# GpSimd subtracts the lower parts of four weight units in VectorE's place

## The chip, the cores and the metric

One core of a Trainium2 chip runs one launch of the kernel. The metric is the device time of that launch in microseconds (us): the median over runs. The engines are called TensorE (PE in the profile), VectorE (DVE), ScalarE (ACT), GpSimd (POOL) and SyncE (SP, which only issues transfers here).

## The reference

Two transformer blocks in sequence over 512 tokens of width 1024, all in float32. The first has a causal pooling branch and a forgetting attention; it is not touched. The second, in which the change lies, is cut here to what matters:

```python
def stick_breaking_attention(q, k, v):           # 8 heads of 64, blocks of 128 queries
    ...
        z = einsum('bqhd,bkhd->bhqk', qb, kb) * scale
        log_beta = log_sigmoid(z)
        log_1m_beta = where(strict, log_sigmoid(-z), 0.0)
        suffix = cumsum(log_1m_beta, axis=3, reverse=True) - log_1m_beta
        w = where(strict, exp(log_beta + suffix), 0.0)
        outs.append(einsum('bhqk,bkhd->bqhd', w, vb))

def second_block(x, c, ...):
    ...
        proj = h @ w_in[l]                       # q, k, v of 8 stick-breaking and 8 chunked heads
        o_sb = stick_breaking_attention(...)
        o_ca = chunked_relpos_attention(...)
        mixed = concatenate([o_sb, o_ca], axis=-1)
        x = x + gt1 * (mixed @ w_o[l])
        h = rmsnorm_2(x, g_norm2[l]) * (1.0 + sc2) + sh2
        x = x + gt2 * (square(relu(h @ w1[l])) @ w2[l])
```

## The kernel before

Every large product is done in three matmuls on split operands: a float32 operand is written as an upper part (rounded to the format that TensorE multiplies) and a lower part (what the rounding left), and `three` (L2276 to L2278) adds upper times upper, upper times lower and lower times upper in one bank of PSUM.

The weights come in 88 units of 128 x 2048, numbered w. SyncE loads a unit into one of three raw buffers (`load`, L575). ScalarE makes the upper part in four chunks of 512 columns (`upper`, L733, semaphore `a["wh"]`), and VectorE subtracts it from the raw chunk to get the lower part (`lower`, L1318, semaphore `v["wl"]`, four counts a unit). There are two homes for the parts, so the upper part of unit w+2 waits until TensorE has read unit w. TensorE waits for the count of `v["wl"]` before the first product of a chunk, and SyncE waits for the fourth count of unit w before it loads another unit into that raw buffer.

Every engine's instructions stand in an order written out by hand. In the stage that matters, steps n run from 0 to 187, sixteen of them to a weight unit (W_CA = 30 at n = 0); in step n of odd index, `slot` puts the chunks of unit w+1 into ScalarE's and VectorE's orders (`UPPER` and `LOWER`, `uppers` and `lowers`). Between the products of the weights lie the "beats" of the attention heads: a score (L2423), its sigmoid on ScalarE (L879), the running product of sticks as a scan on VectorE (`sticks`, L1518, both operands in SBUF), the transposes on TensorE (L2450), the split of the transposed weights on ScalarE (L898) and VectorE (`turned`, L1537, one operand in PSUM), the products with the values (L2474, L2479), and the collection of the head's output (L907, L1548, L916, L1558). A transpose also waits until VectorE's `turned` has emptied its bank, two transposes back. Heads 16 to 23 are the stick-breaking ones.

Units 36 to 39 are the projections of the stick-breaking heads' queries and keys (n = 96 to 159) and units 40 to 43 the output projection (W_O = 40; units 40 and 41 from n = 160 on). Unit 44 is the first of the wide layer that follows.

GpSimd masks scores and loads tiles earlier; in this stage it clears some table corners, builds the strip of the scan (four small instructions up to L2221), and then waits until the last stick-breaking head's values are done (`t["value"]`, `n_turn(23, 0)`) and for ScalarE's sums of squares, to make the factors of the second normalisation (L2227, L2230). Its semaphore `rs1` counts twelve steps of the first normalisation (three for each of four blocks).

Of the kernel before, what the change touches and what calls it, by code (L numbers as in the profile page):

```python
# [17 lines left out]
EPS = 1e-6  # L18
# [121 lines left out]
def program(nc, x, xcols, wall, wf, poolw, params, fng, wada, crow_in, rel, out):  # L140
# [31 lines left out]
    with ExitStack() as ctx:  # L172
# [162 lines left out]

        g = sems("pool_", "const", "meta", "rs0", "rs1", "rs3", "mask", "bt", "strip")

# [160 lines left out]
        def upper_at(w, s_):  # L498
            return uppers.get(w, UPPER).get(s_, ()) if w + 1 < NW else ()

        def lower_at(w, s_):
            return lowers.get(w, LOWER).get(s_, ()) if w + 1 < NW else ()
# [68 lines left out]
        def _(e):  # L571
# [5 lines left out]
            def loads_to(last):  # L577
                while todo[0] <= min(last, W_MLP + 3):
                    n = todo[0]
                    todo[0] += 1  # L580
                    if n >= NR:
                        e.wait_ge(v["wl"], 4 * (n - NR) + 4)
                    load(n, place[n])
# [106 lines left out]
            for q in range(4):  # L690
                o, u, (a0, a1, a2, a3) = W_MLP + 11 * q, W_MLP + 8 * q, places[q]

                if q:
                    e.wait_ge(v["wl"], 4 * o + 4)
                load(u + 4 + 1, a0)
                e.wait_ge(v["wl"], 4 * (o + 1) + 4)
                load(u + 4 + 1, a1)
                e.wait_ge(v["wl"], 4 * (o + 2) + 4)
                load(u + 4, a2)
                e.wait_ge(v["wl"], 4 * (o + 3) + 4)  # L700
                load(u + 4 + 3, a3)
                e.wait_ge(v["wl"], 4 * (o + 5) + 4)
                load(u + 4 + 1, a3)
                if q < 3:
                    e.wait_ge(v["wl"], 4 * (o + 6) + 4)
                    load(u + 8, a0)
                    e.wait_ge(v["wl"], 4 * (o + 8) + 4)
                    load(u + 9, a2)
                    e.wait_ge(v["wl"], 4 * (o + 9) + 4)
                    load(u + 10, a3)  # L710
                    e.wait_ge(v["wl"], 4 * (o + 10) + 4)
                    load(u + 11, a1)
# [8 lines left out]
        def _(e):  # L721
# [312 lines left out]
            def keep(i):  # L1034
                e.wait_ge(g["rs1"], 3 * i + 3)
                e.activation(x1[:, i, :], scaled[:, i % 2, :], ACT.Copy, scale=sm[:, 128 + 2 * i:129 + 2 * i]).then_inc(a["xk"], 1)
# [277 lines left out]
        def _(e):  # L1314
            def lower(w, c):
                e.wait_ge(a["wh"], 4 * w + c + 1)
                upper_, lower_ = parts_at(w, c)
                e.tensor_tensor(lower_, raw_of(w, c), upper_.bitcast(F32), ALU.subtract).then_inc(v["wl"], 1)  # L1318
# [396 lines left out]
            def norms(i):  # L1715

                e.wait_ge(g["rs1"], 3 * i + 3)
                e.wait_ge(t["tp"], i) if i else e.wait_ge(v["ol"], 4)
                e.tensor_scalar(normed, scaled[:, i % 2, :], sm[:, 129 + 2 * i:130 + 2 * i], None,
                                ALU.mult).then_inc(v["xn1"], 1)  # L1720
# [371 lines left out]
        def _(e):  # L2092
# [98 lines left out]
            for i in range(4):  # L2191


                m1, m2 = sm[:, 120 + 2 * i:121 + 2 * i], sm[:, 121 + 2 * i:122 + 2 * i]
                r = sm[:, 128 + 2 * i:130 + 2 * i]
                e.wait_ge(a["nsq"], 2 * i + 1)
                e.tensor_scalar(r[:, 0:1], m1, EPS, None, ALU.add).then_inc(g["rs1"], 1)
                e.wait_ge(a["nsq"], 2 * i + 2)
                e.wait_ge(g["rs1"], 3 * i + 1)
                e.tensor_scalar(r[:, 1:2], r[:, 0:1], EPS, m2, ALU.mult, ALU.add).then_inc(g["rs1"], 1)  # L2200
                e.wait_ge(g["rs1"], 3 * i + 2)
                e.tensor_tensor(r, r, half[:, 0:2], ALU.pow).then_inc(g["rs1"], 1)
            gate(0)
# [3 lines left out]
            for h in CA:  # L2207
                e.wait_ge(d[f"bt{h % 2}"], 16 * (h // 2 - 3))
                e.memset(bt[h % 2][0:64, 448:512], NEG).then_inc(g["bt"], 1)
                if h == 9:  # L2210
                    for j in range(4):
# [9 lines left out]
            e.affine_select(out=strip[:, 384:512], in_=strip[:, 384:512], compare_op=ALU.is_ge, fill=0.0, base=0,  # L2221
                            pattern=[[1, 128]], channel_multiplier=-1).then_inc(g["strip"], 1)
            e.wait_ge(t["value"], n_turn(23, 0))
            for i in range(4):
# [25 lines left out]
            for q in range(4):  # L2250
                o, (a0, a1, a2, a3) = W_MLP + 11 * q + 4, places[q]
                o3, o2 = o + order(q).index(7), o + order(q).index(6)
                if q < 3:
                    e.wait_ge(d[f"w{place[o3]}"], 16 * n_load[o3])
                    add(q, 2, place[o3])
                e.wait_ge(d[f"w{place[o2]}"], 16 * n_load[o2])
                add(q, 2, place[o2])
                e.wait_ge(d[f"wa{place[o2]}"], 192 + 16 * n_add[o2] - 16)
                add(q, 0, place[o2])
                if q == 3:  # L2260
                    e.wait_ge(d[f"w{place[o3]}"], 16 * n_load[o3])
                    add(q, 2, place[o3])
                    to_residual("*c12")
                    to_residual("*c21")
                e.wait_ge(v["wl"], 4 * o + 4)
                add(q, 2, a2)
                e.wait_ge(v["wl"], 4 * o2 + 4)
                add(q, 3, place[o2])
                if q == 0:
                    gate(1)  # L2270
# [3 lines left out]
        def _(e):  # L2274
# [5 lines left out]
            def by_cols(w, sub, k, out_, c0, n, start, stop, fresh):  # L2280

                o = 256 * k + 128 * sub
                upper, lower = home(w)
                if fresh and k % 2 == 0:
                    e.wait_ge(v["wl"], 4 * w + k // 2 + 1)
                return three(out_, upper[:, o:o + 128], lower[:, o:o + 128], hh[:, k, c0:c0 + n],
                             hl[:, k, c0:c0 + n], start, stop)
# [287 lines left out]
            for ee in range(4):  # L2575
# [7 lines left out]
                for i in range(4):  # L2583
                    bank_free(8 * ee + 4 + i)
                    e.wait_ge(v["wl"], 4 * w + i + 1)
                    if ee == 0:
                        e.wait_ge(v["ol"] if i % 2 else v["yl"], 4)
                    for k in range(4):
                        o, kt = 512 * i + 128 * k, 4 * (i % 2) + k
                        ins = three(bank[up_bank(ee, i)], wh[:, w % NH, o:o + 128], wl[:, w % NH, o:o + 128],  # L2590
                                    ah[:, kt, :], al[:, kt, :], k == 0, k == 3)
                    ins.then_inc(t["up"], 1)


            for kh in range(2):
                w = W_OUT + kh
                for i in range(4):
# [4 lines left out]
                    for k in range(4):  # L2602
                        if i == 0:
                            e.wait_ge(v["wl"], 4 * w + k + 1)
                            e.wait_ge(v["ml"], 4 * kh + k + 1)
                        ins = by_rows(w, k, 4 * kh + k, bank[OUT_BANK[0][i]], (mh, ml), 128 * i, 128,
                                      kh == 0 and k == 0, kh == 1 and k == 3)
# [6 lines left out]
            def out_block(i):  # L2614
                if i == 0:
                    e.wait_ge(v["m"], 24)
                for kt in range(8):
                    w = W_OUT + 2 + kt // 4
                    if i == 0:
                        e.wait_ge(v["wl"], 4 * w + kt % 4 + 1)  # L2620
                    ins = by_rows(w, kt % 4, kt, bank[OUT_BANK[1][i]], (mh, ml), 128 * i, 128, kt == 0, kt == 7)
# [14 lines left out]
            def vca_block(i):  # L2636
                for kt in range(8):
                    w = W_VCA + kt // 4
                    if i == 0:
                        e.wait_ge(v["wl"], 4 * w + kt % 4 + 1)  # L2640
                    if kt % 4 == 0:
# [18 lines left out]
            for n in range(steps_s):  # L2660
# [11 lines left out]
                elif n < 96:  # L2672
# [4 lines left out]
                    if i == 0:  # L2677
                        e.wait_ge(v["wl"], 4 * w + kt % 4 + 1)
                    ins = by_rows(w, kt % 4, kt, bank[VSB_BANK[i]], (hh, hl), META + 128 * i, 128, kt == 0, kt == 7)
# [14 lines left out]
                else:  # L2694
# [4 lines left out]
                    if i == 0:  # L2699
                        e.wait_ge(v["wl"], 4 * w + kt % 4 + 1)  # L2700
                        e.wait_ge(v["ol"], 8 if kt > 3 else 9 + kt)
# [17 lines left out]
            e.wait_ge(v["ol"], 12)  # L2719
            e.wait_ge(v["wl"], 4 * (W_O + 1) + 4)  # L2720
            for i in range(4):
# [11 lines left out]
            def o_block(i):  # L2733
                if i == 1:
                    e.wait_ge(v["turn"], n_turn(23, 0))
                for n, kt in enumerate((4, 5, 6, 7, 0, 1, 2, 3)):
                    w = W_O + 2 + (kt < 4)
                    if i == 0:
                        e.wait_ge(v["wl"], 4 * w + kt % 4 + 1)
                    if i == 3 and n == 1:  # L2740
# [32 lines left out]
            def product(q, r):  # L2773
                p, w = ORDER[r], W_MLP + 11 * q + 4 + r
                upper, lower = home(w)
                for b in range(2):
# [5 lines left out]
                    for k in range(4):  # L2782
                        if b == 0:
                            e.wait_ge(v["wl"], 4 * w + k + 1)
                            e.wait_ge(v["sl"], n_sl(q, k if p in (1, 7) else 4 + k, p in (5, 6, 3)))
# [5 lines left out]
            def last_product(r):  # L2791
                p, w = LAST_ORDER[r], W_MLP + 37 + r
                for b in range(2):
# [12 lines left out]
                    for c0, c1 in HALVES[b] if p in (5, 3) else HALVES[0]:  # L2806
                        for k in range(4):
                            if b == 0:
                                e.wait_ge(v["wl"], 4 * w + k + 1)
                                e.wait_ge(v["sl"], n_sl(3, k if p in (1, 7) else 4 + k, p in (5, 6, 3)))  # L2810
# [79 lines left out]
```

## Time and profile before

| what | value |
|---|---|
| median of 3 runs | 955.28 us (955.16 to 955.39) |
| the profiled execution's own time | 955.42 us |
| its span, first to last instruction | 953.7 us |
| TensorE matmul busy | 941.1 us, 4712 instructions |
| VectorE busy | 691.2 us, 1278 instructions |
| ScalarE busy | 565.2 us, 1115 instructions |
| GpSimd busy | 103.8 us, 215 instructions |
| granted TensorE clock | 1.0 |

The page says which engine is busy in which part of the span; the chain of waits says what released what; a timeline gives one instruction a row, with its start and its duration. The durations of matmuls overlap (their ends are modelled), so TensorE is read from the starts of its instructions and from the idle time that the trace lists ahead of one. On VectorE and ScalarE an instruction is listed from its issue, and the next one's start can lie some 0.1 us before the end of the one ahead; back to back, 512-column subtractions start 0.60 us apart.

### The profile page before, as it was taken

To read this page: it belongs to the slowest core of one execution; us is meant where nothing else is said; L and a number is where in the kernel's file an instruction comes from. 1 tells how busy PE (TensorE), PEld (TensorE's weight loads), DVE (VectorE), ACT (ScalarE), POOL (GpSimd) and SP (SyncE) were. 2 spreads that over 40 slices of the span, in tenths; PEclk is the share of its full clock that TensorE was granted. 3 is DMA by queue.
4 is the path that set the end of the run, shared out by engine and by line. 5 is a ranking of instruction groups with operands and counts; after the bars stand their busy time and mean duration, and the time that the engine had idled before them with its cause. 6 is when DMAs were issued, how large, how long until landed. Compare 5 with 4: busy or idle time off the path is not lost.

```text
span 953.7 us, 13305 instructions
## 1 busy us (share of the span) xinstructions
PE 941.1 (99%) x4712; PEld 786.3 (82%) x4712; DVE 691.2 (72%) x1278; ACT 565.2 (59%) x1115; POOL 103.8 (11%) x215
## 2 busy tenths in 40 slices
PE   8999999999999999999999999999999999999998
PEld 7878998888888887877788877898888888888887
DVE  6487888878788766667768886856544853673988
ACT  6448787753223257479987664556745634644562
POOL 5001212211121103000000000110000000000110
PEclk9999999999999999999999999999999999999999
DMA  8233222149798743733442423365867567586773
GB/s 302 89 112 108 69 79 89 55 157 354 284 322 278 190 142 127 300 111 100 133 166 73 127 67 131 146 167 133 212 207 180 168 192 189 122 234 193 169 186 111
DMA packets 34963, 156.71 MB, mean 164 GB/s; under 512 B 5273, under 2 KB 5529, under 8 KB 22226
## 3 DMA queue, kind: packets, MB, share of 16 engines
q1 hardware_dynamic: 21106, 103.64, 31.6%
q0 software_dynamic: 11152, 49.29, 20.9%
q10 hardware_dynamic: 2640, 2.93, 0.9%
q8 instruction: 38, 0.62, 0.3%
q14 instruction: 27, 0.22, 0.1%
HBM read 144.61 MB, written 5.27 MB: 157 GB/s over the span
## 4 chain that ended last, share of the span: by engine, by line
PE 86%; DVE 9%; ACT 3%; issue 1%; DMA 1%; ACTq 0%; POOL 0%; DVEq 0%; POOLq 0%
PE psum L2276 26%; PE psum L2278 25%; PE psum L2277 25%; PE psum L2423 2%; PE psum L2450 2%; PE psum L2479 1%; PE psum L2474 1%; DVE wl L1318 1%; DVE p_sb L1518 1%; DMA raw<-in_wall 1%; DVE ptl L1537 1%; PE psum L2712 1%; DVE hl L1357 1%; DVE xt L1353 1%; DVE ah L1464 1%
## 5 line engine op out<-in xcount | busy, mean ns | idle before, releaser
L2276 PE MATMUL psum<-hh,wh 128*128 128x512 f32 (+2 forms) x736 | 277.7, 377 | 0.7 <-DVE hl L1357 0.6
L2278 PE MATMUL psum<-hh,wl 128*128 128x512 f32 (+2 forms) x736 | 270.2, 367 | 0.0
L2277 PE MATMUL psum<-hl,wh 128*128 128x512 f32 (+2 forms) x736 | 270.0, 367 | 0.0
L1318 DVE TENSOR_TENSOR wl<-raw,wh 128x512 fp32r<-128x512 f32 x336 | 218.7, 685 | 37.6 <-ACT wh L733 37.0
L733 ACT ACTIVATE wh<-raw 128x512 fp32r<-128x512 f32 x336 | 193.3, 621 | 68.3 <-PE psum L2278 65.2
L2276 PEld LDWEIGHTS psum<-hh,wh 128*128 128x128 f32 x736 | 138.5, 188 | 24.5 <-DVE hl L1357 1.8
L2278 PEld LDWEIGHTS psum<-hh,wl 128*128 128x128 f32 x736 | 138.4, 188 | 23.0
L2277 PEld LDWEIGHTS psum<-hl,wh 128*128 128x128 f32 x736 | 138.7, 188 | 20.5 <-issue 1.2
L2276 PE MATMUL psum<-wh,ah 128*128 128x512 f32 x192 | 76.1, 396 | 0.4 <-ACT p_sb L879 0.4
L2278 PE MATMUL psum<-wh,al 128*128 128x512 f32 x192 | 74.9, 390 | 0.0
L2277 PE MATMUL psum<-wl,ah 128*128 128x512 f32 x192 | 74.8, 389 | 0.0
L1221 ACT ACTIVATE two<-psum 128x512 f32<-128x512 f32 x32 | 19.1, 597 | 49.0 <-PE psum L2278 48.9
L2234 POOL DMA_DIRECT2D raw<-in_wall x20 | 17.3, 867 | 252.5 <-DMA raw<-in_wall 142.3
L2450 PE MATMUL psum<-ident,p_sb 128*128 128x128 f32 x240 | 41.6, 274 | 2.0 <-DVE ptl L1537 1.3
L2276 PEld LDWEIGHTS psum<-wh,ah 128*128 128x128 f32 x192 | 36.1, 188 | 8.6 <-issue 1.0
L867 ACT ACTIVATE p_sb<-p_sb,sm 128x528 f32<-128x528 f32 (+3 forms) x64 | 36.2, 566 | 11.2 <-DVE sm L1504 10.5
L2278 PEld LDWEIGHTS psum<-wh,al 128*128 128x128 f32 x192 | 36.0, 188 | 7.7
L2277 PEld LDWEIGHTS psum<-wl,ah 128*128 128x128 f32 x192 | 36.1, 188 | 6.8
L2450 PEld LDWEIGHTS psum<-ident,p_sb 128*128 128x128 f32 x240 | 29.7, 140 | 10.5 <-issue 3.7
L873 ACT ACTIVATE p_sb<-p_sb,sm 128x528 f32<-128x528 f32 (+3 forms) x64 | 35.8, 560 | 0.5 <-DVE sm L1509 0.4
L2278 PE MATMUL psum<-wh,s_y 128*128 128x512 f32 (+1 forms) x92 | 34.9, 380 | 0.0
L1540 DVE TENSOR_TENSOR ptl<-psum,pth 128x128 fp32r<-128x128 f32 (+1 forms) x64 | 30.9, 483 | 2.7 <-ACT pth L901 2.3
(372 smaller groups left out, 1748.6 us busy)
## 6 DMA issues: line engine op xcount, KB each, us to landing
raw<-in_wall SPq DMA_DIRECT2D x79, 1024.0 KB, 5.4
raw<-in_wall POOLq DMA_DIRECT2D x20, 1024.0 KB, 8.1
wa<-in_wada POOLq DMA_DIRECT2D x24, 512.0 KB, 5.8
gt<-in_wada POOLq DMA_DIRECT2D x20, 512.0 KB, 6.9
xt<-in_xcols SPq DMA_DIRECT2D x8, 264.0 KB, 7.9
cb<-c_rows SPq DMA_DIRECT2D x8, 264.0 KB, 3.2
x<-in_x SPq DMA_DIRECT2D x4, 512.0 KB, 11.9
x_kept<-x SPq DMA_DIRECT2D x4, 512.0 KB, 2.6
```

Source lines behind the costliest of these rows:

```text
L733: e.activation(parts_at(w, c)[0], raw_of(w, c), ACT.Copy).then_inc(a["wh"], 1)
L867: e.activation(block_p(h, i), block_p(h, i), ACT.Exp, bias=nmx, scale=1.0 if h in FG else -1.0, accum_out=su).then_inc(a["exp"], 1)
L873: e.activation(block_p(h, i), block_p(h, i), ACT.Copy, scale=mx).then_inc(a["norm"], 1)
L1221: e.activation(two[:, n % 2, :], bank[w1_bank(n)], ACT.Relu).then_inc(a["r"], 1)
L1318: e.tensor_tensor(lower_, raw_of(w, c), upper_.bitcast(F32), ALU.subtract).then_inc(v["wl"], 1)
L1540: e.tensor_tensor(dst, bank[bk][:, 0:w_], ph[:, o:o + w_].bitcast(F32), ALU.subtract).then_inc(v["turn"], 1)
L2234: e.dma_start(raw_at(i), wall[W_MLP + 8 * q + 4 + m], accum_op=ALU.add).then_inc(d[f"wa{i}"], 16)
L2276: e.matmul(out_, lh, rh, start=start, stop=False, skip_group_check=True)
L2277: e.matmul(out_, lh, rl, start=False, stop=False, skip_group_check=True)
L2278: return e.matmul(out_, ll, rh, start=False, stop=stop, skip_group_check=True)
L2423: ins = e.matmul(dst[:, size * j:size * j + size], q[:, 128 * i:128 * i + 128], k[:, size * j:size * j + size], start=k is k_up, stop=k is ...
L2450: ins = e.transpose(bank[bk][:, 128 * (i - i0):128 * (i - i0) + 128], head(h)[0][:, o:o + 128], ident[:, :])
```

## The change

The lower parts of units 38, 39, 40 and 41 (`BY_POOL`) are subtracted by GpSimd: sixteen instructions of 128 x 512, the same operands. They stand in GpSimd's order between the building of the strip (L2221) and the wait for the last values. VectorE's `lower` returns at once for these units. GpSimd counts them on the semaphore of the first normalisation's twelve steps, renamed from `rs1` to `made`, and everyone who waited for a count of `v["wl"]` (TensorE before a chunk's first product, SyncE before a load, GpSimd before its adding transfers) takes semaphore and count from `lows(w, c)`, which takes sixteen from the count of units above 41.

```diff
-        g = sems("pool_", "const", "meta", "rs0", "rs1", "rs3", "mask", "bt", "strip")
+        g = sems("pool_", "const", "meta", "rs0", "made", "rs3", "mask", "bt", "strip")
...
+        BY_POOL = range(W_O - 2, W_O + 2)
+
+        def lows(w, c):
+
+            if w in BY_POOL:
+                return g["made"], 12 + 4 * (w - BY_POOL[0]) + c
+            return v["wl"], 4 * w + c - (16 if w > BY_POOL[0] else 0)
+
...
                     if n >= NR:
-                        e.wait_ge(v["wl"], 4 * (n - NR) + 4)
+                        e.wait_ge(*lows(n - NR, 4))
                     load(n, place[n])
...
             def lower(w, c):
+                if w in BY_POOL:
+                    return
                 e.wait_ge(a["wh"], 4 * w + c + 1)
                 upper_, lower_ = parts_at(w, c)
                 e.tensor_tensor(lower_, raw_of(w, c), upper_.bitcast(F32), ALU.subtract).then_inc(v["wl"], 1)
...
             e.wait_ge(g["strip"], 3)
             e.affine_select(out=strip[:, 384:512], in_=strip[:, 384:512], compare_op=ALU.is_ge, fill=0.0, base=0,
                             pattern=[[1, 128]], channel_multiplier=-1).then_inc(g["strip"], 1)
+            for w in BY_POOL:
+                for c in range(4):
+                    e.wait_ge(a["wh"], 4 * w + c + 1)
+                    upper_, lower_ = parts_at(w, c)
+                    e.tensor_tensor(lower_, raw_of(w, c), upper_.bitcast(F32), ALU.subtract).then_inc(g["made"], 1)
             e.wait_ge(t["value"], n_turn(23, 0))
...
                 if fresh and k % 2 == 0:
-                    e.wait_ge(v["wl"], 4 * w + k // 2 + 1)
+                    e.wait_ge(*lows(w, k // 2 + 1))
```

## Rows read from the trace of the kernel before

**Rows 1.** Stretches: us, busy time of each engine with its instructions, granted clock, DMA.

```profile
486.00:540.00 54.00, 54.00 (x286) 44.95 (x285) 46.24 (x94) 43.18 (x94) 0.24 (x1) 1.00 0.30 98
540.00:582.00 42.00, 39.43 (x218) 31.58 (x216) 37.06 (x62) 27.41 (x60) 0.00 (x0) 1.00 0.31 94
```

**Rows 2.** TensorE's waits from 540 to 582: us in total, times, longest.

```profile
PE psum L2450 <- DVE ptl L1537: 1.3, 2, 0.7
PE psum L2474 <- DVE ptl L1537: 0.6, 1, 0.6
```

**Rows 3.** Chain that ended last, 542.4 to 549.3: start, us, what.

```profile
545.44 0.60 DVE wl L1318
```

**Rows 4.** Timeline of VectorE, 552 to 570: start, us, instruction.

```profile
552.41 1.23 DVE L1518 TENSOR_TENSOR_SCAN p_sb<-p_sb,rows 128x512 f32<-128x512 f32 x1
...
554.01 0.95 DVE L1518 TENSOR_TENSOR_SCAN p_sb<-p_sb,rows 128x384 f32<-128x384 f32 x1
...
563.45 0.96 DVE L1518 TENSOR_TENSOR_SCAN p_sb<-p_sb,rows 128x384 f32<-128x384 f32 x1
...
564.91 0.68 DVE L1518 TENSOR_TENSOR_SCAN p_sb<-p_sb,rows 128x256 f32<-128x256 f32 x1
565.51 0.67 DVE L1318 TENSOR_TENSOR wl<-raw,wh 128x512 fp32r<-128x512 f32 x1
566.09 0.69 DVE L1537 SCALAR_TENSOR_TENSOR ptl<-psum,pth 128x512 fp32r<-128x512 f32 x1
...
569.58 1.23 DVE L1518 TENSOR_TENSOR_SCAN p_sb<-p_sb,rows 128x512 f32<-128x512 f32 x1 [0.52 <-ACT p_sb L879]
```

**Rows 5.** Timeline of TensorE, 566 to 570.

```profile
566.17 0.34 PE L2474 MATMUL psum<-ptl,v_sb 128*64 128x384 f32 x1
566.35 0.34 PE L2479 MATMUL psum<-pth,v_sb 128*128 128x384 f32 x1
566.83 0.44 PE L2474 MATMUL psum<-ptl,v_sb 128*64 128x512 f32 x1
...
569.48 0.48 PE L2276 MATMUL psum<-wh,ah 128*128 128x512 f32 x1
```

**Rows 6.** Timeline of ScalarE, the uppers from 551 to 569.

```profile
551.76 0.62 ACT L733 ACTIVATE wh<-raw 128x512 fp32r<-128x512 f32 x1
...
562.30 0.63 ACT L733 ACTIVATE wh<-raw 128x512 fp32r<-128x512 f32 x1
...
564.26 0.64 ACT L733 ACTIVATE wh<-raw 128x512 fp32r<-128x512 f32 x1
...
564.94 0.65 ACT L733 ACTIVATE wh<-raw 128x512 fp32r<-128x512 f32 x1
...
568.43 0.62 ACT L733 ACTIVATE wh<-raw 128x512 fp32r<-128x512 f32 x1
```

**Rows 7.** Groups by line, GpSimd, whole span.

```profile
L2110 POOL MEMSET v<- 128x1024 f32 x1 | 1.0, 955 | 0.0
...
L2135 POOL MEMSET pth<- 128x512 f32 x1 | 0.5, 532 | 0.1
...
L2221 POOL TENSOR_SCALAR_AFFINE_SELECT rows<-rows 128x128 f32<-128x128 f32 x1 | 0.3, 293 | 0.1
```

**Rows 8.** Timelines of GpSimd and VectorE, 81 to 97.

```profile
82.22 0.60 POOL L2141 TENSOR_SCALAR_AFFINE_SELECT p_sb<-p_sb 128x128 f32<-128x128 f32 x1 [11.30 <-DVE p_sb L1489]
...
95.06 0.29 POOL L2141 TENSOR_SCALAR_AFFINE_SELECT p_sb<-p_sb 128x128 f32<-128x128 f32 x1 [4.16 <-DVE p_sb L1489]
...
81.30 0.77 DVE L1489 SCALAR_TENSOR_TENSOR p_sb<-psum,ccol,cb 128x528 f32<-128x528 f32 x1 [1.69 <-PE psum L2423]
81.98 0.68 DVE L1318 TENSOR_TENSOR wl<-raw,wh 128x512 fp32r<-128x512 f32 x1
...
95.16 0.73 DVE L1318 TENSOR_TENSOR wl<-raw,wh 128x512 fp32r<-128x512 f32 x1
```

**Rows 9.** Timeline of GpSimd, 486.5 to 611.

```profile
604.88 0.30 POOL L2227 TENSOR_SCALAR sm<-sm 128x1 f32<-128x1 f32 x1 [118.65 <-ACT sgt L1175]
```

More of the change, by code:

```diff
@@ L693, in _ @@
                 if q:
-                    e.wait_ge(v["wl"], 4 * o + 4)
+                    e.wait_ge(*lows(o, 4))
                 load(u + 4 + 1, a0)
-                e.wait_ge(v["wl"], 4 * (o + 1) + 4)
+                e.wait_ge(*lows(o + 1, 4))
                 load(u + 4 + 1, a1)
-                e.wait_ge(v["wl"], 4 * (o + 2) + 4)
+                e.wait_ge(*lows(o + 2, 4))
                 load(u + 4, a2)
-                e.wait_ge(v["wl"], 4 * (o + 3) + 4)
+                e.wait_ge(*lows(o + 3, 4))
                 load(u + 4 + 3, a3)
-                e.wait_ge(v["wl"], 4 * (o + 5) + 4)
+                e.wait_ge(*lows(o + 5, 4))
                 load(u + 4 + 1, a3)
                 if q < 3:
-                    e.wait_ge(v["wl"], 4 * (o + 6) + 4)
+                    e.wait_ge(*lows(o + 6, 4))
                     load(u + 8, a0)
-                    e.wait_ge(v["wl"], 4 * (o + 8) + 4)
+                    e.wait_ge(*lows(o + 8, 4))
                     load(u + 9, a2)
-                    e.wait_ge(v["wl"], 4 * (o + 9) + 4)
+                    e.wait_ge(*lows(o + 9, 4))
                     load(u + 10, a3)
-                    e.wait_ge(v["wl"], 4 * (o + 10) + 4)
+                    e.wait_ge(*lows(o + 10, 4))
                     load(u + 11, a1)
@@ L1034, in keep @@
             def keep(i):
-                e.wait_ge(g["rs1"], 3 * i + 3)
+                e.wait_ge(g["made"], 3 * i + 3)
                 e.activation(x1[:, i, :], scaled[:, i % 2, :], ACT.Copy, scale=sm[:, 128 + 2 * i:129 + 2 * i]).then_inc(a["xk"], 1)
@@ L1715, in norms @@
             def norms(i):
-                e.wait_ge(g["rs1"], 3 * i + 3)
+                e.wait_ge(g["made"], 3 * i + 3)
                 e.wait_ge(t["tp"], i) if i else e.wait_ge(v["ol"], 4)
@@ L2196, in _ @@
                 e.wait_ge(a["nsq"], 2 * i + 1)
-                e.tensor_scalar(r[:, 0:1], m1, EPS, None, ALU.add).then_inc(g["rs1"], 1)
+                e.tensor_scalar(r[:, 0:1], m1, EPS, None, ALU.add).then_inc(g["made"], 1)
                 e.wait_ge(a["nsq"], 2 * i + 2)
[L2199 to L2202, printed above, removed]
+                e.wait_ge(g["made"], 3 * i + 1)
+                e.tensor_scalar(r[:, 1:2], r[:, 0:1], EPS, m2, ALU.mult, ALU.add).then_inc(g["made"], 1)
+                e.wait_ge(g["made"], 3 * i + 2)
+                e.tensor_tensor(r, r, half[:, 0:2], ALU.pow).then_inc(g["made"], 1)
             gate(0)
@@ L2264, in _ @@
                     to_residual("*c21")
-                e.wait_ge(v["wl"], 4 * o + 4)
+                e.wait_ge(*lows(o, 4))
                 add(q, 2, a2)
-                e.wait_ge(v["wl"], 4 * o2 + 4)
+                e.wait_ge(*lows(o2, 4))
                 add(q, 3, place[o2])
@@ L2584, in _ @@
                     bank_free(8 * ee + 4 + i)
-                    e.wait_ge(v["wl"], 4 * w + i + 1)
+                    e.wait_ge(*lows(w, i + 1))
                     if ee == 0:
@@ L2603, in _ @@
                         if i == 0:
-                            e.wait_ge(v["wl"], 4 * w + k + 1)
+                            e.wait_ge(*lows(w, k + 1))
                             e.wait_ge(v["ml"], 4 * kh + k + 1)
@@ L2619, in out_block @@
                     if i == 0:
-                        e.wait_ge(v["wl"], 4 * w + kt % 4 + 1)
+                        e.wait_ge(*lows(w, kt % 4 + 1))
                     ins = by_rows(w, kt % 4, kt, bank[OUT_BANK[1][i]], (mh, ml), 128 * i, 128, kt == 0, kt == 7)
@@ L2639, in vca_block @@
                     if i == 0:
-                        e.wait_ge(v["wl"], 4 * w + kt % 4 + 1)
+                        e.wait_ge(*lows(w, kt % 4 + 1))
                     if kt % 4 == 0:
@@ L2677, in _ @@
                     if i == 0:
-                        e.wait_ge(v["wl"], 4 * w + kt % 4 + 1)
+                        e.wait_ge(*lows(w, kt % 4 + 1))
                     ins = by_rows(w, kt % 4, kt, bank[VSB_BANK[i]], (hh, hl), META + 128 * i, 128, kt == 0, kt == 7)
@@ L2699, in _ @@
                     if i == 0:
-                        e.wait_ge(v["wl"], 4 * w + kt % 4 + 1)
+                        e.wait_ge(*lows(w, kt % 4 + 1))
                         e.wait_ge(v["ol"], 8 if kt > 3 else 9 + kt)
@@ L2719, in _ @@
             e.wait_ge(v["ol"], 12)
-            e.wait_ge(v["wl"], 4 * (W_O + 1) + 4)
+            e.wait_ge(*lows(W_O + 1, 4))
             for i in range(4):
@@ L2738, in o_block @@
                     if i == 0:
-                        e.wait_ge(v["wl"], 4 * w + kt % 4 + 1)
+                        e.wait_ge(*lows(w, kt % 4 + 1))
                     if i == 3 and n == 1:
@@ L2783, in product @@
                         if b == 0:
-                            e.wait_ge(v["wl"], 4 * w + k + 1)
+                            e.wait_ge(*lows(w, k + 1))
                             e.wait_ge(v["sl"], n_sl(q, k if p in (1, 7) else 4 + k, p in (5, 6, 3)))
@@ L2808, in last_product @@
                             if b == 0:
-                                e.wait_ge(v["wl"], 4 * w + k + 1)
+                                e.wait_ge(*lows(w, k + 1))
                                 e.wait_ge(v["sl"], n_sl(3, k if p in (1, 7) else 4 + k, p in (5, 6, 3)))
```

## The prediction

> **What bounds the kernel now.** I read the stretches first. From 486 to 540 us, in which the lower parts of units 38 and 39 are made, TensorE is busy in all of its 54.00 us; from 540 to 582, with those of units 40 and 41, in 39.43 of 42.00, while VectorE is busy in 37.06 [rows 1]. The granted clock is 1.00 in both, so nothing in the sum hangs on it. Then the waits: what TensorE stands still for from 540 to 582 is VectorE's `turned` (L1537), 1.9 us of the 2.57 [rows 2]. Then the chain, to see what VectorE did just before: an instruction that is taken away pays only where it stands between the last arrival from another engine and the `turned` that TensorE waits for. So VectorE's busy time is not what the change is worth; its place in four or five short chains is.
>
> **What goes, and what it pays.** Sixteen subtractions leave VectorE, 0.68 us each (as the one at 81.98 [rows 8]), 10.9 in all, of which 0.60 each counts on the chain [rows 3].
> - Eight of them (units 38, 39) lie where TensorE has no idle time [rows 1]: worth nothing.
> - Of unit 40's four, one is a link of the chain, at 545.44 for 0.60, ahead of the `turned` that TensorE waits 0.6 us for [rows 2, 3]. That wait (A) goes: -0.60. What is late next there is TensorE's own stream. The other three stand behind a `turned` and before VectorE waits for ScalarE anyway: nothing.
> - Of unit 41's four, one stands between the scan at 564.91 and the `turned` at 566.09 (0.58 from start to start), and TensorE takes the product of that piece at 566.83, 0.48 after the 384-column one at 566.35, where the 384-column one before it was followed after 0.18 (C) [rows 4, 5]. That is 0.30: -0.30. The other three are not ahead of a wait.
>
> Three more waits lie in this stretch, two of them the longest (0.7 and 0.6, the two of L2450) [rows 2]; ahead of them stand scans, sigmoids and `turned`, no subtraction, and they stay. Sum of what goes: -0.9 us.
>
> **What comes, and where it hides.** GpSimd has nothing to do up to 604.88, 118.65 us of waiting [rows 9]. The trace shows no subtraction of this size on it. A memset of 512 columns takes 0.53 us, of 1024 0.96: 0.83 ns a column and 0.11 fixed; a 128-column instruction that reads and writes takes 0.29, 1.4 ns a column [rows 7]. With one read that makes 0.11 + 512 x 1.4 = 0.84 us, with the second read fully added 1.27 (0.42 more). The bounds are 0.53 (a write alone) and 1.6 (everything twice); I take 1.1, between the two readings.
>
> Does it come in time? GpSimd starts a chunk as soon as ScalarE has made its upper part, where VectorE's slots came later. Unit 41's first chunk has its upper part at 562.93 [rows 6]; its first product begins at 569.48 [rows 5], so an instruction of up to 6 us would do. The other units have more room: their chunks are a whole unit's products ahead. The twelve counts before it are long past, and GpSimd's instructions behind it (the factors from 604.88 on) stay where they were. SyncE's waits for a free raw buffer end earlier, which moves only unit 44's load forward by some us; it is used after 600. ScalarE waits for no lower part. So the arithmetic itself hides, and the instructions cost nothing by themselves.
>
> **What it can cost: VectorE and GpSimd getting in each other's way.** An instruction of GpSimd that reads SBUF took 0.60 us at 82.22 while VectorE ran a subtraction with both operands in SBUF (81.98 to 82.66), against 0.29 at 95.06, beside an instruction with one operand in PSUM; of the 32 of this form, eleven took some 0.6 and each of them stood beside an instruction with two operands in SBUF [rows 8]. GpSimd waits for the whole of such an instruction. The other way round: the subtraction at 95.16, which started 0.10 us into GpSimd's, took 0.73 instead of 0.68 [rows 8]. It was let go at about 95.21, half-way through GpSimd's 0.29. So VectorE waits too, for at least the time in which GpSimd reads. The new instructions read 2 x 512 columns; at 0.83 ns a column [rows 7] they keep VectorE's two-operand instructions out for 0.85 us. Bounds: 0.05 a meeting, as in the two of this kind (one stands here), and 1.27, all of the longer reading. I take 0.85. In the critical stretch the instructions with two operands in SBUF are the scans.
>
> The meetings that stand on a chain (GpSimd's start taken 0.15 behind the release, as at 82.22 behind 82.07 [rows 8]):
> - B: unit 40's last upper part ends at 551.78 once A has gone (552.38 less 0.60) [rows 6]; the 512-column scan starts at 551.81 and is ahead [rows 4]. GpSimd reads from its end, 553.04, to 553.89; the 384-column scan, due at 553.41, starts 0.48 late, and so does the `turned` for which TensorE already waits a little: +0.48.
> - C: unit 41's first chunk is read from 563.08 to 563.93; the scan due at 563.45 is 0.48 late. The second chunk (upper part at 564.90) is read from 565.05 to 565.90; the 256-column scan, due at 564.91 + 0.48 = 565.39, starts at 565.90, 0.99 late. The subtraction that stood there (0.58) is gone: the `turned` comes 0.41 later than before, so C's -0.30 is not won but turned into +0.41.
> - D: unit 41's last chunk is released at 569.05 and read from 569.20 to 570.05; the scan at 569.58 [rows 4], ahead of TensorE's wait of 0.6, is 0.47 late: +0.47.
> - Other meetings, with units 38 and 39 and the first chunks of unit 40, fall where TensorE has no wait or VectorE is waiting for ScalarE: nothing.
>
> **Sum:** -0.60 + 0.48 + 0.41 + 0.47 = +0.76 us. The profiled execution took 955.42, its span 953.7, and the median is 955.28; on the median this makes 956.0. After 582 TensorE works without a gap again, and the shift is carried to the end.
>
> The Trainium skill states (SBUF — State Buffer, Who interferes with whom) that a VectorE instruction with two inputs in SBUF contends with a GpSimd instruction that reads SBUF, and that the later of the two blocks fully until the first is through; it speaks against the change. The rows agree for GpSimd's side (0.60 against 0.29); for VectorE's side they show 0.05. Another page (GPSIMD Engine Reference, Elementwise — side-by-side cycle accounting) gives 4497 ns for 2048 columns; a quarter of it, an estimate, is 1.12 us. By the two together the sum would be about +1.7; by the 0.05 alone, about -0.7.
>
> **The rivals.**
> 1. *VectorE is not held up* (0.05 a meeting, as at 95.16). Then only the two links count: -0.9 + 4 x 0.05 = -0.7, 954.6 us. For it: the two meetings shown. Against: GpSimd had little left to read there.
> 2. *Two of GpSimd's instructions in a row ahead of one scan* (the other side: slower). Unit 41's third chunk is released at 565.59 [rows 6], so it stands ready when the second is done at 565.90, exactly when the scan waits. If GpSimd's next goes first, C costs another 0.85; if the scan at B loses its lead of 0.12 us, B costs 551.93 + 0.85 - 551.81 = 0.97 instead of 0.48. Sum: 0.76 + 0.85 + 0.49 = +2.1, 957.4 us. It decides as soon as the third chunk is released before the waiting scan gets in.
> 3. *All waits go*: with VectorE less loaded TensorE loses all of its 2.57 us of idle time [rows 1]: 952.7. Against: two of the long waits have no subtraction ahead of them.
> 4. *GpSimd too slow*: TensorE or the loads wait for the lower part. It needs over 6 us an instruction, four times my upper bound; at 8 us, unit 41's first chunk would be 1.6 us late and the second 7 more: some 964.
>
> **How the numbers follow.** The forecast, 956.0, has a chance of 0.50, with a range of its own from 955.2 (half of the hold) to 957.1 (a hold of 1.27); rival 1 0.27, rival 2 0.18, rival 3 0.03, rival 4 0.02. Within 0.2% (1.9 us, about what a measurement of this kernel can tell from no change) is 953.4 to 957.2. Faster by more is rival 3 and a little: 0.04. Slower by more are rivals 2 and 4: 0.20. The rest, 0.76, is the same. The range of 8 in 10 goes from rival 1 with a little to spare, 954.2, to rival 2, 957.5.
>
> **What would show it.** Right: sixteen GpSimd subtractions of about 1.1 us, some longer by a VectorE instruction; scans longer than 1.23, 0.95 and 0.68 or starting late beside them; no wait at the first chain (A), longer waits at the other three. Wrong: scans of the old length beside GpSimd's reads (rival 1), TensorE waiting for a lower part (rival 4), a scan late by two of GpSimd's instructions (rival 2), or waits elsewhere, above all before 540, where I count nothing.

## The result, and the profile after

The changed kernel takes 957.59 us (median of 12 runs, 957.26 to 958.15), the kernel before 955.49 (12 runs, 955.16 to 955.98): 1.0022 of it, with an interval of [1.0014, 1.003]. It is slower by 2.1 us; the forecast was 0.7 us slower, 956.0, in a range up to 957.5. The profiled executions have 957.62 us with a span of 955.9, against 955.42 with 953.7.

Three things show where the time went. First the page's line of busy time (us, share of the span, instructions):

```profile
PE 941.5 (98%) x4712; PEld 786.3 (82%) x4712; DVE 688.4 (72%) x1262; ACT 564.9 (59%) x1115; POOL 126.3 (13%) x231
```

and two stretches (us, then busy time and instructions of TensorE, its weight loads, VectorE, ScalarE and GpSimd, granted clock, DMA share and GB/s):

```profile
486.00:540.00 54.00, 53.49 (x284) 44.36 (x283) 44.80 (x88) 42.41 (x93) 10.98 (x8) 1.00 0.31 98
540.00:584.00 44.00, 40.08 (x221) 32.22 (x220) 35.79 (x54) 28.14 (x61) 11.65 (x8) 1.00 0.32 96
```

Sixteen subtractions have left VectorE, yet its busy time has fallen by 2.8 us (from 691.2) and not by 10.9: what is left on it takes longer. The clock is 1.00 in both stretches. TensorE, busy in all of 486 to 540 before [rows 1], now stands still there for 0.51 us, and from 540 to 584 for 3.92 (2.57 in the kernel before, over the same 44 us as over the 42 of rows 1). Second, TensorE's waits from 500 to 600 (us in total, times, longest), with those of before in rows 2:

```profile
PE psum L2465 <- DVE ptl L1547: 2.5, 3, 1.3
PE psum L2489 <- DVE ptl L1547: 1.4, 2, 0.8
```

L2465 is the transpose (L2450 before), L2489 the product with the values (L2474), L1547 the `turned` (L1537). The transposes' waits have grown from 1.3 to 2.5 us and are three instead of two; the products' from 0.6 to 1.4. GpSimd's lower parts (L2237) end no wait of TensorE. Third, the new instructions. As a group by line (count, us together, mean ns of one, idle time before):

```profile
L2237 POOL TENSOR_TENSOR wl<-raw,wh 128x512 fp32r<-128x512 f32 x16 | 22.6, 1421 | 63.5 <-ACT wh L741 63.5
```

as the instructions of that line (count, shortest, median and longest in ns, when):

```profile
L2237 POOL TENSOR_TENSOR wl<-raw,wh x16: 1283/1292/2257, 509.7 to 570.6; 128x512 fp32r<-128x512 f32 x16
```

and the five whose meetings matter, in the timeline of GpSimd (start, us, instruction, idle time before and what ended it):

```profile
533.68 1.28 POOL L2237 TENSOR_TENSOR wl<-raw,wh 128x512 fp32r<-128x512 f32 x1 [4.80 <-ACT wh L741]
...
552.68 2.26 POOL L2237 TENSOR_TENSOR wl<-raw,wh 128x512 fp32r<-128x512 f32 x1 [3.44 <-ACT wh L741]
563.79 1.29 POOL L2237 TENSOR_TENSOR wl<-raw,wh 128x512 fp32r<-128x512 f32 x1 [8.85 <-ACT wh L741]
565.77 1.30 POOL L2237 TENSOR_TENSOR wl<-raw,wh 128x512 fp32r<-128x512 f32 x1 [0.69 <-ACT wh L741]
...
570.55 1.29 POOL L2237 TENSOR_TENSOR wl<-raw,wh 128x512 fp32r<-128x512 f32 x1 [1.87 <-ACT wh L741]
```

And what VectorE did beside them, in its timeline:

```profile
534.10 1.95 DVE L1528 TENSOR_TENSOR_SCAN p_sb<-p_sb,rows 128x512 f32<-128x512 f32 x1
536.08 0.42 DVE L1547 SCALAR_TENSOR_TENSOR ptl<-psum,pth 128x256 fp32r<-128x256 f32 x1
...
552.63 1.23 DVE L1528 TENSOR_TENSOR_SCAN p_sb<-p_sb,rows 128x512 f32<-128x512 f32 x1
554.23 1.53 DVE L1528 TENSOR_TENSOR_SCAN p_sb<-p_sb,rows 128x384 f32<-128x384 f32 x1
...
564.24 1.66 DVE L1528 TENSOR_TENSOR_SCAN p_sb<-p_sb,rows 128x384 f32<-128x384 f32 x1
566.40 1.21 DVE L1528 TENSOR_TENSOR_SCAN p_sb<-p_sb,rows 128x256 f32<-128x256 f32 x1
...
571.00 1.93 DVE L1528 TENSOR_TENSOR_SCAN p_sb<-p_sb,rows 128x512 f32<-128x512 f32 x1 [0.52 <-ACT p_sb L887]
```

Scans of 512, 384 and 256 columns take 1.23, 0.95 or 0.96, and 0.68 us in the kernel before [rows 4]. Each scan that meets a subtraction of GpSimd already under way is longer. Its length beyond the usual one tells when it was let go, that is, when it could begin its work: 571.00 + (1.93 - 1.23) = 571.70, which is 1.15 after GpSimd's start at 570.55; 564.24 + 0.70 = 564.94, 1.15 after 563.79; 534.10 + 0.72 = 534.82, 1.14 after 533.68; 566.40 + 0.53 = 566.93, 1.16 after 565.77. So a subtraction of 1.29 us keeps a scan out for 1.15; below this is called the hold. The other way round GpSimd's at 552.68, behind a scan that had started 0.05 earlier, took 2.26. It ended at 554.94, 1.08 behind the scan's end at 553.86, so it waited for the scan, with some 0.2 of its own 1.29 us spent beside it. The next scan, at 554.23, was 0.58 longer than 0.95 and so let go at 554.81: behind the scan's end the hold is only 0.95.

To price the waits I took, from the starts of TensorE's instructions, each step's length (from one start to the next) beyond what its columns take: 0.23 us for 512 columns or for two instructions of 256, 0.17 for 384. The places are named as in the prediction; N is new.

| place (us) | before | after | difference | forecast |
|---|---|---|---|---|
| N, transposes of head pieces at 536 | 0 | 0.67 | +0.67 | 0 |
| A, product at 547.6 | 0.78 | 0.23 | -0.55 | -0.60 |
| B, at 556 | 0.24 | 0.79 | +0.55 | +0.48 |
| C, at 566 to 567 | 0.31 | 0.94 | +0.63 | +0.41 |
| D, at 570 to 572 | 0.76 | 1.49 | +0.73 | +0.47 |
| sum | | | +2.03 | +0.76 |

The rows for C after (those before are in rows 5), then for D before and after, in TensorE's timeline:

```profile
567.14 0.34 PE L2494 MATMUL psum<-pth,v_sb 128*128 128x384 f32 x1
568.25 0.45 PE L2489 MATMUL psum<-ptl,v_sb 128*64 128x512 f32 x1 [0.77 <-DVE ptl L1547]
...
570.26 0.40 PE L2423 MATMUL psum<-v_ca 128*128 128x256 f32 x2
571.26 0.63 PE L2450 MATMUL psum<-ident,p_sb 128*128 128x128 f32 x4 [0.60 <-DVE ptl L1537]
...
571.67 0.40 PE L2438 MATMUL psum<-v_ca 128*128 128x256 f32 x2
573.39 0.63 PE L2465 MATMUL psum<-ident,p_sb 128*128 128x128 f32 x4 [1.32 <-DVE ptl L1547]
```

The whole can be read in one more way: the same instruction of TensorE begins 0.09 us later than in the kernel before at 500 us, 2.12 later at 600, and 2.20 later at 950. So the loss arises between 500 and 600 and is carried to the end. The sum of the table is that growth of 2.03, and the measured 2.1 us within 0.1.

### The profile page after: what moved, and what is told of

Same layout as the page of the kernel before. It is cut to its first block, busy times and chain, and to the rows that moved or that the text cites. A ratio compares the mean times of both kernels' runs of the same rounds, so it can differ in the third digit from the quotient of the medians.

```text
span 955.9 us, 13305 instructions
## 1 busy us (share of the span) xinstructions
PE 941.5 (98%) x4712; PEld 786.3 (82%) x4712; DVE 688.4 (72%) x1262; ACT 564.9 (59%) x1115; POOL 126.3 (13%) x231
## 4 chain that ended last, share of the span: by engine, by line
PE 85%; DVE 9%; ACT 3%; issue 1%; DMA 1%; SPq 0%; POOL 0%; DVEq 0%; ACTq 0%; POOLq 0%
PE psum L2291 25%; PE psum L2293 25%; PE psum L2292 25%; PE psum L2438 2%; PE psum L2465 2%; DVE p_sb L1528 2%; PE psum L2494 1%; PE psum L2489 1%; DVE wl L1328 1%; DMA raw<-in_wall 1%; DVE ptl L1547 1%; PE psum L2727 1%; DVE hl L1367 1%; DVE xt L1363 1%; DVE ah L1474 1%
## 5 line engine op out<-in xcount | busy, mean ns | idle before, releaser
L1328 DVE TENSOR_TENSOR wl<-raw,wh 128x512 fp32r<-128x512 f32 x320 | 207.9, 685 | 37.7 <-ACT wh L741 37.0
L2465 PE MATMUL psum<-ident,p_sb 128*128 128x128 f32 x240 | 41.5, 273 | 3.2 <-DVE ptl L1547 2.5
L2465 PEld LDWEIGHTS psum<-ident,p_sb 128*128 128x128 f32 x240 | 29.7, 140 | 11.9 <-issue 3.7
L1528 DVE TENSOR_TENSOR_SCAN p_sb<-p_sb,rows 128x512 f32<-128x512 f32 (+3 forms) x32 | 31.0, 974 | 3.4 <-ACT p_sb L887 3.4
```

The costliest lines, as they stand in the source:

```text
L1528: e.tensor_tensor_scan(p[:, ::-1], p[:, ::-1], whole[:, ::-1], 0.0, ALU.mult, ALU.max).then_inc(v["scan_s"], 1)
L2465: ins = e.transpose(bank[bk][:, 128 * (i - i0):128 * (i - i0) + 128], head(h)[0][:, o:o + 128], ident[:, :])
```

## The experiments

The theory: VectorE's scans are kept out while GpSimd reads, at four places (N, B, C and D) on chains that end in TensorE. A rival: the new waits and the moved order, or GpSimd's work as such, cost the time. The kernel before took 955.50 to 955.64 us beside these runs (medians of 15 runs or more).

**GpSimd writes but doesn't read.** Everything stays, waits and order too, only the subtraction becomes a memset of the same size (the lower parts of units 38 to 41 are left out).

```diff
-                    e.tensor_tensor(lower_, raw_of(w, c), upper_.bitcast(F32), ALU.subtract).then_inc(g["made"], 1)
+                    e.memset(lower_.bitcast(F32), 0.0).then_inc(g["made"], 1)
```

> The changed kernel, but GpSimd fills the sixteen lower parts with zeros instead of subtracting (the lower parts of units 38 to 41 are thus left out of the result). Same order, same counts, same 512-column writes, no reads. Theory 1 (VectorE's scans wait while GpSimd READS the SBUF): scans at their own lengths again (1.23, 0.95, 0.68 us), TensorE's waits at 535.9, and the growth of those at 556.5, 567.1 and 571.8, gone; only what was won stays (about 0.6 + 0.3): 954.6 us, 0.9 under before. Theory 2 (it is the order, the counts, an earlier load, or GpSimd being at work at all): near the changed kernel, 957.5.

Measured: 954.60 us, 0.9991 [0.9982, 1.0]; 3.0 us below the changed kernel. TensorE's waits on VectorE from 500 to 600:

```profile
PE psum L2465 <- DVE ptl L1547: 1.3, 2, 0.7
```

The transposes' waits are those of before. N, the growth at B and D, and the product's waits at A and C are gone. In the timeline of VectorE and GpSimd the two run side by side, each at its own length:

```profile
551.80 1.23 DVE L1528 TENSOR_TENSOR_SCAN p_sb<-p_sb,rows 128x512 f32<-128x512 f32 x1
551.83 0.53 POOL L2237 MEMSET wl<- 128x512 f32 x1 [4.22 <-ACT wh L741]
```

So what costs the time lies in the subtraction's reads or its length, and neither in the waits nor in the order. The Trainium skill (SBUF — State Buffer, Who interferes with whom) says that a VectorE instruction with two inputs in SBUF contends with a GpSimd instruction that reads SBUF and not with one that only writes it; this run and the next agree (0.53 us beside a scan here, 1.60 there).

**GpSimd reads one operand.** The subtraction becomes a copy of the raw chunk (the lower parts of units 38 to 41 are left out, and the raw weights stand in their place).

```diff
-                    e.tensor_tensor(lower_, raw_of(w, c), upper_.bitcast(F32), ALU.subtract).then_inc(g["made"], 1)
+                    e.tensor_copy(lower_, raw_of(w, c)).then_inc(g["made"], 1)
```

> The changed kernel, but GpSimd copies the raw chunk into the lower part (one read instead of two; the lower parts of units 38 to 41 are thus wrong in the result). Theory 1: an instruction of some 0.7 to 0.9 us, which keeps a scan out for its reading time, some 0.5 to 0.75 instead of the 1.15 seen: each of the four late scans is some 0.5 less late, so 955.0 to 956.0. Theory 2: 957.5.

Measured: 954.73 us, 0.9991 [0.9982, 1.0], below the expected 955.0 to 956.0. The timeline of GpSimd and VectorE:

```profile
533.65 0.62 POOL L2237 CAST wl<-raw 128x512 fp32r<-128x512 f32 x1 [5.50 <-ACT wh L741]
...
534.08 1.26 DVE L1528 TENSOR_TENSOR_SCAN p_sb<-p_sb,rows 128x512 f32<-128x512 f32 x1
...
551.91 1.22 DVE L1528 TENSOR_TENSOR_SCAN p_sb<-p_sb,rows 128x512 f32<-128x512 f32 x1
551.94 1.60 POOL L2237 CAST wl<-raw 128x512 fp32r<-128x512 f32 x1 [4.08 <-ACT wh L741]
```

A copy is done in 0.62 us, and the scan at 534.08 was let go 0.03 late, at 534.11: 0.46 after the copy's start. At that length the scans on the chains are hardly met. The copy takes less than half of the subtraction's 1.29 us, and I had expected a longer one. What the copy does show is that it waits behind a scan (1.60 at 551.94) where the memset at 551.83 did not: the reads are what meets.

**One pair of units alone.** First only units 38 and 39, then only 40 and 41; the offset in `lows` becomes `4 * len(BY_POOL)`.

```diff
-        BY_POOL = range(W_O - 2, W_O + 2)
+        BY_POOL = range(W_O - 2, W_O)
```

> Only the two projection units (38, 39) go to GpSimd, VectorE keeps 40 and 41. Theory 1: only one chain is met there, the last chunk of unit 39 and the 512-column scan at 534.1, whose delay TensorE feels as 0.67 at 535.9; nothing is won: 955.4 + 0.7 = 956.1. A cost that is spread over all sixteen would give half of the whole, 956.5, with no single wait.

```diff
-        BY_POOL = range(W_O - 2, W_O + 2)
+        BY_POOL = range(W_O, W_O + 2)
```

> Only the two output units (40, 41) go to GpSimd, VectorE keeps 38 and 39. Theory 1: the first wait goes (-0.55), the three later ones grow by 0.55, 0.63 and 0.73: 955.4 + 1.4 = 956.8, and no wait at 535.9. A cost spread over all sixteen: 956.5.

Measured: 956.37 us, 1.0009 [0.9999, 1.0018], and 956.94, 1.0014 [1.0004, 1.0024]. TensorE's waits from 500 to 600 with units 38 and 39 alone:

```profile
PE psum L2465 <- DVE ptl L1547: 1.8, 3, 0.7
PE psum L2489 <- DVE ptl L1547: 0.6, 1, 0.6
```

and with 40 and 41 alone:

```profile
PE psum L2465 <- DVE ptl L1547: 2.0, 2, 1.3
PE psum L2489 <- DVE ptl L1547: 1.4, 2, 0.8
```

The first pair has the third transposes' wait (N, 0.69) and nothing else new: +0.8 us from the units that I had put at nothing. The second has A, B, C and D as in the changed kernel (0.22, 0.78, 0.94, 1.49) and no N: +1.4. Together they are +2.2, the whole of the loss.

**Two chunks given back.** The last chunks of units 39 and 41, which meet the scans at N and D, go back to VectorE (`BY_POOL` becomes a list of chunks).

```diff
+        BY_POOL = [(w_, c_) for w_ in range(W_O - 2, W_O + 2) for c_ in range(4) if (w_, c_) not in ((W_O - 1, 3), (W_O + 1, 3))]
...
-                if w in BY_POOL:
+                if (w, c) in BY_POOL:
                     return
```

> The changed kernel with two of its sixteen chunks given back to VectorE: the last of unit 39 and the last of unit 41, whose subtractions on GpSimd keep out the 512-column scans at 534.1 and 571.0. Theory 1: TensorE's wait at 535.9 goes (-0.67) and that at 571.8 falls back from 1.49 to 0.77 (-0.72); the waits at 556.5 and 567.1 stay: 957.6 - 1.4 = 956.2 us. A cost spread over all sixteen: 957.6 - 2.1 x 2/16 = 957.3.

Measured: 956.05 us, 1.0006 [0.9997, 1.0015]. TensorE's waits from 500 to 600:

```profile
PE psum L2489 <- DVE ptl L1548: 1.4, 2, 0.8
PE psum L2465 <- DVE ptl L1548: 1.3, 2, 0.7
```

N is gone and D is back at 0.76, while B (0.78) and C (0.94) stay: two of sixteen instructions carry 1.5 of the 2.1 us.

**Only chunks that meet nothing.** GpSimd keeps unit 38 and the first three chunks of units 39 and 40.

```diff
+        BY_POOL = [(w_, c_) for w_ in range(W_O - 2, W_O + 2) for c_ in range(4) if w_ <= W_O and (w_ < W_O - 1 or c_ < 3)]
```

> GpSimd keeps the ten chunks that meet no scan on a chain (unit 38, the first three of 39 and the first three of 40); VectorE has the last of 39, the last of 40 and unit 41 again. Theory 1: nothing of the cost is left and the wait at the first chain is won (-0.55): 954.9 us, under the kernel before. Spread over all: 955.5 + 10/16 of 2.1 = 956.8.

Measured: 955.30 us, 0.9998 [0.9989, 1.0007], 0.4 above what was expected. The trace has the steps that were expected (A 0.22, B 0.23, C 0.31, D 0.78): against the kernel before the same instruction of TensorE begins 0.32 us earlier at 500 us, before any subtraction of GpSimd, and 0.87 earlier at 600, so 0.55 is gained between. Its spans show it too: their median is 953.2 us against 953.8 for the kernel before beside it. What is missing lies outside the span: in every run of this kernel the time is 2.05 to 2.10 us above the span, in every run of the others 1.68 to 1.78. Why that is so isn't shown. So the expected gain is there, and some 0.35 us outside the span take most of it back.

**The order alone, without GpSimd.** The kernel before, all sixteen subtractions on VectorE, but the first one of unit 40 and the first one of unit 41 moved to later slots, out of the chains of A and C.

```diff
+        lowers[W_O - 1] = {4: (0, 1), 6: (2,), 7: (3,)}
+        lowers[W_O] = {2: (0, 1), 4: (2,), 5: (3,)}
```

> The kernel before, GpSimd without part in it: VectorE makes the first lower part of unit 40 two slots later and that of unit 41 one slot later, behind the piece that TensorE waits for. Theory 1 with its reading of the chains: the same two links are taken out, without any meeting: -0.55 and -0.3, 954.6 us, as with the memset. If it is VectorE's load as such (10.9 us less busy) that gave the memset kernel its gain, this one stays at 955.5.

Measured: 954.61 us, 0.9991 [0.9982, 1.0]. The stretch from 540 to 584, with the columns of above:

```profile
540.00:584.00 44.00, 42.12 (x232) 34.10 (x231) 38.23 (x65) 28.71 (x63) 0.00 (x0) 1.00 0.30 96
```

TensorE's waits on VectorE from 500 to 600:

```profile
PE psum L2452 <- DVE ptl L1539: 1.3, 2, 0.7
```

And a part of the chain that ended last (start, us, what):

```profile
545.42 0.87 DVE p_sb L1520
...
547.34 0.58 DVE ptl L1539
...
548.25 1.18 DVE wl L1320 x2
```

The subtraction that stood at 545.44 [rows 3] now comes behind the `turned` at 547.34, and the scan is at 545.42 in its place. The waits at A and C are gone as with the memset, with GpSimd idle and VectorE as busy as before (its page has 691.2 us). What the change could win was an order on VectorE and not its load.

**Subtractions in halves.** Two instructions of 256 columns for each of 512.

```diff
-                    e.tensor_tensor(lower_, raw_of(w, c), upper_.bitcast(F32), ALU.subtract).then_inc(g["made"], 1)
+                    for h in range(2):
+                        o = slice(256 * h, 256 * h + 256)
+                        ins = e.tensor_tensor(lower_[:, o], raw_of(w, c)[:, o], upper_.bitcast(F32)[:, o], ALU.subtract)
+                    ins.then_inc(g["made"], 1)
```

> The changed kernel with each of GpSimd's subtractions cut into two of 256 columns (the same work, 32 instructions of about 0.7 us, reading for about 0.6). Theory 1, with the hold lasting one instruction and a waiting scan going in between the two: delays of 0.15 to 0.25 in place of 0.55 to 0.72: waits at 535.9 about 0.15, at 556.5 about 0.6, at 567.1 about 0.3, at 571.8 about 0.95: 955.6 us. If GpSimd's next instruction goes ahead of a waiting scan: as the changed kernel, 957.5 or more.

Measured: 955.41 us, 1.0 [0.9992, 1.0009]; 2.2 below the changed kernel. The scan at D, and GpSimd's two halves ahead of it (the timeline of both engines, the halves in one row):

```profile
568.17 2.33 POOL L2239 TENSOR_TENSOR wl<-raw,wh 128x256 fp32r<-128x256 f32 x2 [0.20 <-ACT wh L741]
...
568.62 1.37 DVE L1528 TENSOR_TENSOR_SCAN p_sb<-p_sb,rows 128x512 f32<-128x512 f32 x1 [0.52 <-ACT p_sb L887]
```

The scan took 0.14 more than 1.23 instead of 0.70 more: it was let go at 568.76, 0.59 after the first half's start, went ahead of the second half, and the second half waited. The hold is half as long because the instruction is shorter, with the same data read and more load on GpSimd, not less (its page has 134.4 us of busy time against 126.3). C is gone and N is down to 0.12 (expected 0.15), A is 0.21 and B 0.30; D is left at 0.91, and the step behind it is 0.15 longer than before. How much under the kernel before this form comes stays open: its trace gains 0.39 us between 500 and 600, but its runs go from 954.83 to 956.23 and their median is only 0.1 below.

**One more order.** The last kernel of VectorE alone, with ScalarE's last upper part of unit 41 a slot later, so that it isn't ahead of the sigmoid on D's chain.

```diff
         lowers[W_O - 1] = {4: (0, 1), 6: (2,), 7: (3,)}
         lowers[W_O] = {2: (0, 1), 4: (2,), 5: (3,)}
+        uppers[W_O] = {0: (0,), 1: (1,), 2: (2,), 4: (3,)}
```

> The reordered kernel (e7_order), and ScalarE makes the last upper part of unit 41 one slot later, out of the chain through the sigmoid at 568.0 to the scan at 568.6, whose piece TensorE waits 0.6 for at 570. Theory 1 (an instruction pays where it stands ahead of a wait, on whatever engine): the sigmoid starts as soon as the score is there, about 0.25 earlier, and the wait at 570 shrinks by as much: 954.6 - 0.25 = 954.4 us. If the score itself ends last there: 954.6.

Measured: 954.43 us (954.20 to 955.06), 0.9987 [0.9978, 0.9996]: faster than the kernel before and than the changed one. D fell from 0.76 to 0.64, by 0.12 where 0.25 was expected, because the sigmoid is now late by something else; ScalarE's timeline:

```profile
568.33 0.60 ACT L882 ACTIVATE p_sb<-psum 128x512 f32<-128x512 f32 x1 [0.29 <-PE psum L2426]
```

It waits 0.29 us for TensorE's score. Against the version without this line the median is 0.2 lower, but the profiled span 0.3 longer (953.1 against 952.8). The trace tells where that comes from: this execution was already 0.44 us behind the kernel before at 500 us, ahead of any changed instruction, where the other's was 0.06 ahead. From 500 to 600 it gains 1.05 us and the other 0.88. So the steps speak for a further 0.2 us, though the medians' intervals overlap.

## Why the prediction was right and wrong

**What held.** The mechanism and its places: the eight subtractions of units 40 and 41 win A (-0.55, forecast -0.60) and lose at B, C and D because scans wait while GpSimd reads. The 0.30 at C is won without the hold (with the memset), and more than given back with it. No one waits for a lower part, so rival 4 is out. Rival 3, all waits gone, is out too: the two long ones have grown.

**The first step that failed: "Other meetings, with units 38 and 39 ..., fall where TensorE has no wait ...: nothing".** This is +0.67 of the missing 1.27 us. I took a TensorE without idle time to have time to spare, and the one doesn't follow from the other. Here are the rows of the kernel before that I should have read, VectorE's timeline and then TensorE's:

```profile
534.01 1.23 DVE L1518 TENSOR_TENSOR_SCAN p_sb<-p_sb,rows 128x512 f32<-128x512 f32 x1
...
535.26 0.42 DVE L1537 SCALAR_TENSOR_TENSOR ptl<-psum,pth 128x256 fp32r<-128x256 f32 x1
...
535.86 0.38 PE L2450 MATMUL psum<-ident,p_sb 128*128 128x128 f32 x2
```

The `turned` that frees the transposes' bank ended at 535.68, and the transpose began at 535.86. In the changed kernel it begins 0.15 behind such a release: `turned` from 536.08 for 0.42 ends at 536.50, and TensorE's timeline has

```profile
535.74 0.40 PE L2438 MATMUL psum<-v_ca 128*128 128x256 f32 x2
536.65 0.52 PE L2465 MATMUL psum<-ident,p_sb 128*128 128x128 f32 x3 [0.51 <-DVE ptl L1547]
```

So there were 0.03 us of slack, and a scan that was 0.72 late cost nearly all of it. The meeting itself could have been found by the same working as B, C and D. Of the others of units 38 and 39 the forecast was right: a scan at 527.74 took 1.68 us beside GpSimd, and TensorE doesn't wait there.

**The second: the hold, taken as 0.85, is 1.15.** The memset's 0.83 ns a column for two operands gave 0.85; the instruction took 1.29 instead of 1.1, and all but its last 0.14 is closed to the scans. This is a mis-sized term: B, C and D are 0.07, 0.22 and 0.26 above their forecasts, 0.55 together. B is least off because GpSimd waited there behind a scan, and only 0.95 of the hold lay behind that scan's end. The rest, 0.05, is A. The prediction's own range for the hold was not worked through the three places, either: a hold of 1.27, put in for 0.85 at B, C and D, makes +2.0 and 957.3, not 957.1 (with N's 0.67 it would have been 958.0), and half the hold makes 954.8, or 954.5 if the second scan at C then isn't met at all, not 955.2. The copy, whose hold of 0.46 is about that half, took 954.73.

The Trainium skill (GPSIMD Engine Reference, Elementwise — side-by-side cycle accounting) led to an estimate of 1.12 us for the instruction; measured are 1.29. The Trainium skill's rule that the later one blocks fully (SBUF — State Buffer, Who interferes with whom) is what the scans show, up to 0.14 us before the end. The sum by both (put in for 0.85 it makes +1.6, where the prediction says about +1.7) was nearer than mine.

**Rival 1** (no hold, 954.6) is what the memset gave, 954.60, by taking the reads away: its price was right and its condition false. **Rival 2** was nearest in time (957.4), and its mechanism did not occur. At C the scan at 566.40 was waiting while GpSimd's third subtraction stood ready (ScalarE had made its upper part by 566.38); the timeline of GpSimd has for that one

```profile
567.02 1.66 POOL L2237 TENSOR_TENSOR wl<-raw,wh 128x512 fp32r<-128x512 f32 x1
```

0.37 us longer than alone: the scan went in between. At B the scan kept a lead of 0.05 us (552.63 against 552.68). So the upper end of the range, 957.5, stood on a rival that wasn't there, and that the time comes so near it is luck: it's the sum of two other errors.

## What to carry to other kernels

Ask of an instruction that is to be moved where it stands in the short chains ahead of the bound engine's waits, and not what load it takes away: here a new order on the same engine won 0.9 us and the move lost 2.1. Where another engine has no idle time, price the slack from the rows (end of what it needs to start of what needs it) before calling a delay there free. An instruction of GpSimd that reads two operands from SBUF keeps out VectorE's scans, which have both operands there, for nearly its whole length (1.15 of 1.29 us). So put it where no scan on a chain is due, or cut it in halves, which gave back 2.2 us here.

## What the runs showed of the hardware

- The hold shows as a longer duration of the waiting scan and not as a later start (1.93 for 1.23), so it hides in VectorE's busy time.
- It lasts 1.15 of the 1.29 us of a subtraction, 0.46 of the 0.62 of a copy, 0.59 for a half of 256 columns, and was not seen with a memset (0.53).
- A waiting scan goes between two of GpSimd's instructions that are queued back to back (566.40 between 565.77 and 567.02; 568.62 between two halves).
- At 512 columns GpSimd takes 0.62 us for the copy of one operand and 1.29 for the subtraction of two.
- Not only scans are held: in the kernel with halves VectorE's subtraction `al` (both operands in SBUF, 0.68 us in the kernel before) took 1.17 us at 511.98, where GpSimd's second half ended at 512.61. The prediction had named the scans alone as instructions of this kind.
